# Expert jobs of 96 row slots, and four neighbouring rows of the experts' second matrix per partition

## The chip, the cores and the metric

The kernel runs on one core of a Trainium2 chip. The metric is the device time of one execution in microseconds; the median of several runs is compared. The core has a tensor engine (TensorE, "PE" in the profile, with its loads of stationary operands shown apart as "PEld"), a vector engine (VectorE, "DVE"), a scalar engine (ScalarE, "ACT"), GpSimd ("POOL") and SyncE ("SP"), which here only issues transfers. Sixteen DMA engines move data between HBM and the on-chip memory (SBUF, 128 partitions).

## The reference, cut to what matters

One step of a two-layer decoder on 256 prompt rows and 8 sample rows of width 1024, all in f32. Layer 0 is an HGRN2 recurrence followed by a dense SwiGLU with 3584 inner columns. Layer 1 is a short gated convolution followed by a SwiGLU of 8 experts, of which each row uses two:

```python
def moe_swiglu(x, router, w1, w3, w2):
    logits = (xt @ router).astype(F32)
    top_v, top_i = lax.top_k(logits, TOP_K)          # TOP_K = 2 of 8
    gates = jax.nn.softmax(top_v, axis=-1)
    combine = jnp.sum(jax.nn.one_hot(top_i, N_EXPERTS, dtype=F32) * gates[..., None], axis=1)
    for e in range(N_EXPERTS):
        out = out + combine[:, e:e + 1] * swiglu(xt, w1[e], w3[e], w2[e]).astype(F32)
```

`swiglu(x, w1, w3, w2)` is `(silu(x @ w1) * (x @ w3)) @ w2`, with `w1` and `w3` of 1024 x 3584 and `w2` of 3584 x 1024. A residual sum and a last RMSNorm follow.

## The kernel before

Every weight passes once from HBM through `raw` (three buffers of 128 x 4096 f32, each in two halves) and is split by ScalarE into a high part `whi` (line 887 in the expert stage) and by VectorE into a low part `wlo` (line 1020), both fp32r. A product then is three matmuls: high by high, high by low, low by high. A piece is half a buffer, 128 x 2048. SP issues the load of a half (line 332) as soon as the low part of that half's last content is made. The expert stage keeps six pieces split ahead; the semaphore `used` counts those that TensorE has done with.

The expert stage routes the 264 rows, gives each row a rank within each of its two experts, and scatters the normed rows into `xg_rows` in HBM (GpSimd, line 582), where each expert has `SLOTS = 3 * P` row slots: three jobs of up to 128 rows. `jobs` (line 290) runs the first job of each expert in order, eight in all; a second or third job is run only where `flag` says that an expert has more than 128 or 256 rows (lines 1609 to 1612). Both HBM buffers, `xg_rows` and `y_rows`, are filled with zeros beforehand, in twelve transfers issued by SP between the weight loads of the dense SwiGLU (`zero_rows`, line 403).

A job on TensorE: the rows of the job are loaded as `xg`, eight transposes (`turn_rows`, line 2130) put them into PSUM with the model columns on the partitions, ScalarE and VectorE copy them out as `xgh` and `xgl` (lines 926, 1576). For the first expert the rows come instead from matmuls with a selection matrix `pm` (line 2101). Then seven blocks of 512 inner columns follow. In each, `up_m` runs twice (banks 0 and 1, for `w1` and `w3`): 24 matmuls with `xgh` or `xgl` stationary and 512 columns of a weight piece moving (lines 2120 to 2122). ScalarE makes `hs = silu` (line 942), VectorE `hx = hs * bank 1` (line 1639), four transposes turn `hx` (`turn`, line 2151; `hx` stationary, the identity moving), ScalarE and VectorE copy the result out as `hth` and `htl` (lines 959, 1655), and `down_m` runs 24 matmuls with these stationary and 512 columns of the `w2` piece moving (line 2166), which add up in two banks over the whole job. TensorE's order is written out so that the transposes of a block stand between the two `up_m` of the next. At the end of a job ScalarE copies the sum into `ybuf` (line 987) and writes it to `y_rows`; after the last job GpSimd gathers each row's two results (line 590), and VectorE and ScalarE combine and norm them (lines 1688 to 1699).

Of the kernel before, what the change touches and what calls it, by code (L numbers as in the profile page):

```python
# [32 lines left out]
def build(nc, x_prompt, x_sample, state_hgrn, state_conv, norm_mix, norm_ffn, norm_final,  # L33
# [29 lines left out]
    SLOTS = 3 * P  # L63
# [8 lines left out]
    with ExitStack() as ctx:  # L72
# [78 lines left out]
        for g_ in range(2):  # L151
# [30 lines left out]
            R0, ("xs", [P, TT, D], F32), ("xgh", [P, DT, P], F32R), ("xgl", [P, DT, P], F32R),  # L182
            ("xg", [P, D], F32), ("hs", [P, FW], F32), ("hx", [P, FW], F32),
            ("hth", [P, 4, P], F32R), ("htl", [P, 4, P], F32R))
# [6 lines left out]
            ("cnt", [P, E], F32), ("flag", [P, NS + 8], I32), ("idx", [P, 2, TT], I32), ("pm", [P, TT, P], F32))  # L191
# [10 lines left out]
        assert FILL * (FB - 1) == E * SLOTS and FILL % (2 * P) == 0  # L202
# [87 lines left out]
        def jobs(eng, head, body):  # L290

            head(0, 0, 0)
            with eng.Fori(0, E - 1) as e:
                body(e, e, e * SLOTS, True)
            body(E - 1, E - 1, (E - 1) * SLOTS, False)  # L300
            more = eng.value_load(flag[0:1, NS:NS + 1], min_val=0, max_val=1)
            with eng.If(more > 0):
                count = eng.alloc_register("jobs_done")
                eng.reg_mov(count, E)
                with eng.Fori(1, 3) as c:
                    with eng.Fori(0, E) as e:
                        col = c * E + e
                        here = eng.value_load(flag[0:1, bass.ds(col, 1)], min_val=0, max_val=1)
                        with eng.If(here > 0):
                            k = eng.snap(count, min_val=E, max_val=3 * E)  # L310
                            head(k, e, e * SLOTS + c * P)
                            body(k, e, e * SLOTS + c * P, False)
                            eng.reg_add(count, count, 1)
                            eng.nop()
                        eng.end_ifs()
                        eng.nop()
            eng.end_ifs()
# [3 lines left out]
        def _(sp):  # L321
# [79 lines left out]
            def zero_rows(dst, i):  # L401

                sp.dma_start(dst[bass.ds(i * FILL, FILL), :].rearrange("(p r s) n -> p r (s n)", p=P, s=2),
                             zeros[:, :].unsqueeze(1).to_broadcast([P, FILL // P // 2, 2 * D])
                             ).then_inc(sem("zero_filled"), 16)
# [20 lines left out]

            def rows_in(k, row):
                sp.wait_ge(sem("dispatched"), 2 * TT * 16)
                sp.wait_ge(sem("xg_turned"), k)
                sp.dma_start(xg[:, :], xg_rows[bass.ds(row, P), :]).then_inc(sem("xg_loaded"), 16)  # L430
# [9 lines left out]
            def body(k, e, row, ahead):  # L440

                n = k * JOB + C_MOE
                with sp.Fori(0, FB - 1) as i:
                    m = n + i * 3 + 2
                    cols = bass.ds(i * FW + FW, FW)
                    chunk(m, expert(moe_w1, e, 0, DT)[:, :, cols], 2)
                    chunk(m + 1, expert(moe_w3, e, 0, DT)[:, :, cols], 0)
                    chunk(m + 2, expert(moe_w2, e, i * 4, 4), 1)
                if ahead:
# [3 lines left out]
                    chunk(n + (JOB + 1), expert(moe_w2, e, 4 * (FB - 1), 4), 1)  # L453
                else:
                    chunk(n + (JOB - 1), expert(moe_w2, e, 4 * (FB - 1), 4), 2)
# [141 lines left out]
        def _(act):  # L597
# [324 lines left out]
            def gathered(k):  # L922
# [3 lines left out]
                a.activation(xgh[:, :, :].rearrange("p (j d) s -> p j (d s)", j=2), Q[1][:, 2:4, :],  # L926
# [12 lines left out]
            def silu(nth, last):  # L939
                act.wait_ge(used, last)  # L940
                act.wait_ge(sem("hx_ready"), nth + 1)
                a.activation(hs[:, :], Q[0][:, 0, :], ACT.Silu).then_inc(sem("hs_ready"), 1)
# [9 lines left out]
            def body(k, e, row, ahead):  # L952
# [34 lines left out]
                a.activation(ybuf[:, :].rearrange("p (j n) -> p j n", j=2), Q[1][:, 0:2, :], ACT.Copy  # L987
                             ).then_inc(sem("y_copied"), 1)
                act.wait_ge(sem("y_copied"), k + 2)
                act.dma_start(y_rows[bass.ds(row, P), :], ybuf[:, :]).then_inc(sem("y_stored"), 16)  # L990
# [17 lines left out]
        def _(dve):  # L1008
# [564 lines left out]
            def gathered(k):  # L1573
# [3 lines left out]
                                Q[1][:, 2:4, :],  # L1577
# [7 lines left out]
            for t in range(TT):  # L1585
                v.tensor_scalar(pm[:, t, :], iota[:, :], 1.0, tk[:, 13, t:t + 1], ALU.add, ALU.is_equal
# [21 lines left out]
            for c in (1, 2):  # L1608
                then(v.tensor_scalar(flag[:, c * E:(c + 1) * E], cnt[:, :], float(P * c), None,
                                     ALU.is_gt))  # L1610
            then(v.tensor_reduce(tk[:, 2, 0:1], cnt[:, :], AX.X, ALU.max))
            then(v.tensor_scalar(flag[:, NS:NS + 1], tk[:, 2, 0:1], float(P), None, ALU.is_gt))
# [23 lines left out]
            def mul(nth, last):  # L1636
                dve.wait_ge(used, last)
                dve.wait_ge(sem("hs_ready"), nth + 1)
                v.tensor_tensor(hx[:, :], hs[:, :], Q[0][:, 1, :], ALU.mult
# [9 lines left out]
            def body(k, e, row, ahead):  # L1649
# [3 lines left out]
                def low(nth):  # L1653
                    dve.wait_ge(sem("hth_ready"), nth + 1)
                    v.tensor_tensor(htl[:, :, :].rearrange("p a s -> p (a s)"), Q[0][:, 2, :],  # L1655
# [49 lines left out]
        def _(pe):  # L1705
# [391 lines left out]
            for t in range(TT):  # L2097
                r = rows[t]
                pe.wait_ge(sem("xs_ready"), t + 1)
                for d in range(DT):  # L2100
                    mm = t_.matmul(Q[1][:, 2 + d // 4, P * (d % 4):P * (d % 4 + 1)],  # L2101
# [133 lines left out]
```

## Time and profile before

| | us |
|---|---|
| median of three runs | 1589.92 |
| lowest and highest | 1587.15, 1593.22 |
| the profiled execution | 1587.53 |
| its span, first to last instruction | 1585.8 |

| engine | busy in the span |
|---|---|
| TensorE matmul | 1499.7 us, 95% |
| TensorE loads | 1307.8 us, 82% |
| VectorE | 1239.5 us, 78% |
| ScalarE | 954.3 us, 60% |
| GpSimd | 66.5 us, 4% |
| DMA | 484.49 MB, mean 306 GB/s |

A row of the profile names the line, the engine, the operation, the tile written and those read, and their shapes. For a matmul the tiles read are the moving one first and the stationary one second; a load (`LDWEIGHTS`) names the same. The duration of one matmul (about 0.39 us) is longer than the distance to the next (0.23 us), since they are pipelined: the distance is what counts. The chain of waits goes back from the last instruction and gives each piece the time that it added to the end. Waits tell for whom an engine stood idle. Windows give busy time by stretch; "PEclk" is the granted share of TensorE's 2.4 GHz.

### The profile page before, as it was taken

Reading aid. Unit: us, or ns where it says so; the run is one execution under the profiler, and the core shown is the slowest. Engines: PE = TensorE matmul, PEld = TensorE weight load, DVE = VectorE, ACT = ScalarE, POOL = GpSimd, SP = SyncE. Lnnn points to the kernel's source line nnn. Section 1 sums busy time; section 2 is a strip of 40 time slices with the busy share of each in tenths; the row PEclk is TensorE's granted clock in tenths of the full one; section 3 lists DMA queues with packets and bytes.
Section 4 is the critical chain, followed back from the end, with each engine's and each line's share of the span. In section 5 each row is a group of like instructions: output and inputs, shape, how many; then the busy total and the mean of one; then the engine's idle time right before and its main releaser. Section 6 shows DMA issues by size and latency. Waiting matters only on the chain.

```text
span 1585.8 us, 23285 instructions
## 1 busy us (share of the span) xinstructions
PE 1499.7 (95%) x8758; PEld 1307.8 (82%) x8759; DVE 1239.5 (78%) x886; ACT 954.3 (60%) x671; POOL 66.5 (4%) x61
## 2 busy tenths in 40 slices
PE   6998699999989979999999999999999999999992
PEld 5987689999979978888888888888888888888881
DVE  5898665655657759888888888888888888888883
ACT  4644244334334347777777777777777777777761
POOL 1033400000000011000000000000000000000001
PEclk9999899999989989999999999999999999999997
DMA  7645377888726539999999999999999999999962
GB/s 269 194 154 163 124 280 268 297 312 312 248 102 200 167 99 400 395 393 374 377 380 370 377 379 370 377 384 360 389 375 362 383 382 357 385 381 362 380 240 96
DMA packets 212938, 484.49 MB, mean 306 GB/s; under 512 B 8810, under 2 KB 26314, under 8 KB 209820
## 3 DMA queue, kind: packets, MB, share of 16 engines
q1 hardware_dynamic: 209080, 473.67, 82.4%
q10 hardware_dynamic: 2532, 5.84, 1.0%
q0 software_dynamic: 1280, 4.33, 0.7%
q8 instruction: 33, 0.54, 0.1%
q14 instruction: 13, 0.11, 0.0%
HBM read 446.45 MB, written 37.40 MB: 305 GB/s over the span
## 4 chain that ended last, share of the span: by engine, by line
PE 82%; DVE 4%; issue 1%; ACT 1%; DMA 1%; POOL 0%; POOLq 0%; ACTq 0%; DVEq 0%
PE Q L2166 20%; PE Q L2122 13%; PE Q L2120 13%; PE Q L2121 13%; PE Q L1737 7%; PE Q L1738 7%; PE Q L1739 7%; PE Q L2151 2%; DVE wlo L1020 1%; DVE sr L1054 0%; PE Q L2101 0%; DMA back<-y_rows,idx 0%; PE Q L2130 0%; DVE xl L1046 0%; DVE xn L1041 0%
## 5 line engine op out<-in xcount | busy, mean ns | idle before, releaser
L1020 DVE TENSOR_TENSOR wlo<-raw,whi 128x2048 fp32r<-128x2048 f32 x414 | 940.3, 2289 | 207.0 <-ACT whi L887 121.1
L887 ACT ACTIVATE whi<-raw 128x2048 fp32r<-128x2048 f32 x336 | 643.1, 1921 | 185.0 <-PE Q L2122 85.4
L2120 PE MATMUL Q<-whi,xgh 128*128 128x512 f32 x896 | 357.5, 399 | 2.4 <-issue 2.4
L2122 PE MATMUL Q<-whi,xgl 128*128 128x512 f32 x896 | 353.8, 395 | 0.0
L2121 PE MATMUL Q<-wlo,xgh 128*128 128x512 f32 x896 | 352.8, 394 | 0.0
L1737 PE MATMUL Q<-xh,whi 128*128 128x264 f32 x1024 | 298.3, 291 | 14.7 <-DVE xl L1046 6.3
L1738 PE MATMUL Q<-xl,whi 128*128 128x264 f32 x1024 | 295.5, 289 | 0.0
L1739 PE MATMUL Q<-xh,wlo 128*128 128x264 f32 x1024 | 294.1, 287 | 0.0
L1737 PEld LDWEIGHTS Q<-xh,whi 128*128 128x128 f32 x1024 | 197.4, 193 | 17.4 <-issue 15.6
L2120 PEld LDWEIGHTS Q<-whi,xgh 128*128 128x128 f32 x896 | 169.3, 189 | 38.1 <-issue 2.6
L2122 PEld LDWEIGHTS Q<-whi,xgl 128*128 128x128 f32 x896 | 169.2, 189 | 37.6
L2121 PEld LDWEIGHTS Q<-wlo,xgh 128*128 128x128 f32 x896 | 169.3, 189 | 36.6
L1738 PEld LDWEIGHTS Q<-xl,whi 128*128 128x128 f32 x1024 | 197.4, 193 | 0.4
L1739 PEld LDWEIGHTS Q<-xh,wlo 128*128 128x128 f32 x1024 | 196.8, 192 | 0.0
L2166 PE MATMUL Q<-whi,hth 128*128 128x512 f32 x448 | 176.3, 393 | 1.4 <-DVE htl L1655 1.4
L2166 PE MATMUL Q<-whi,htl 128*128 128x512 f32 x448 | 177.0, 395 | 0.0
L2166 PE MATMUL Q<-wlo,hth 128*128 128x512 f32 x448 | 176.0, 393 | 0.0
L608 ACT ACTIVATE whi<-raw 128x2048 fp32r<-128x2048 f32 x42 | 80.0, 1912 | 86.0 <-PE Q L1739 83.7
L823 ACT ACTIVATE whi<-raw 128x2048 fp32r<-128x2048 f32 x36 | 68.8, 1911 | 90.2 <-PE Q L1739 90.2
L2166 PEld LDWEIGHTS Q<-whi,hth 128*128 128x128 f32 x448 | 84.5, 189 | 20.0 <-DVE htl L1655 1.6
L2166 PEld LDWEIGHTS Q<-wlo,hth 128*128 128x128 f32 x448 | 84.2, 188 | 19.3
L2166 PEld LDWEIGHTS Q<-whi,htl 128*128 128x128 f32 x448 | 84.4, 188 | 18.4
(231 smaller groups left out, 1099.1 us busy)
## 6 DMA issues: line engine op xcount, KB each, us to landing
raw<-in_moe_w SPq DMA_DIRECT2D x336, 1024.0 KB, 7.6
raw<-in_ffn_w SPq DMA_DIRECT2D x42, 1024.0 KB, 6.9
raw<-in_hgrn_w_in SPq DMA_DIRECT2D x16, 1024.0 KB, 6.4
xg_rows<-zeros SPq DMA_DIRECT2D x6, 2048.0 KB, 10.8
y_rows<-zeros SPq DMA_DIRECT2D x6, 2048.0 KB, 10.8
raw<-in_conv_w_in SPq DMA_DIRECT2D x12, 1024.0 KB, 6.0
st<-in_state_hgrn SPq DMA_DIRECT2D x8, 512.0 KB, 4.4
raw<-in_hgrn_w_out SPq DMA_DIRECT2D x4, 1024.0 KB, 5.1
```

Of the source, the lines that this page charges most:

```text
L608: a.activation(whi[:, buf, :], raw[:, slot, PW * half:PW * (half + 1)], ACT.Copy).then_inc(hi_done, 1)
L823: a.activation(whi[:, base % SPLIT, :], raw[:, n % RAW, PW * (base % 2):PW * (base % 2 + 1)], ACT.Copy).then_inc(hi_done, 1)
L887: a.activation(bufs(q)[0], raw[:, n % RAW, PW * (q % 2):PW * (q % 2 + 1)], ACT.Copy).then_inc(hi_done, 1)
L1020: v.tensor_tensor(low, raw[:, slot, PW * half:PW * (half + 1)], high.bitcast(F32), ALU.subtract).then_inc(lo_done, 1)
L1737: t_.matmul(out, w[wslice], xhi, start=start, stop=False, **kw)
L1738: t_.matmul(out, w[wslice], xlo, start=False, stop=False, **kw)
L1739: return t_.matmul(out, lo[wslice], xhi, start=False, stop=stop, **kw)
L2120: t_.matmul(out, xgh[:, kt, :], high[:, w], start=(kt == 0), stop=False)
L2121: t_.matmul(out, xgh[:, kt, :], low[:, w], start=False, stop=False)
L2122: mm = t_.matmul(out, xgl[:, kt, :], high[:, w], start=False, stop=(kt == DT - 1))
L2151: mm = t_.transpose(Q[0][:, 2, P * c:P * (c + 1)], hx[:, P * c:P * (c + 1)], ident[:, :])
L2166: mm = t_.matmul(out, lhs[:, f, :], rhs[:, w], start=(begin and f == 0 and lhs is hth and rhs is high), stop=(last and f == 3 and lhs is h ...
```

## The change

A job has 96 row slots in place of 128 (`CAP`). `SLOTS` becomes 288, a job's rows lie `c * CAP` behind the expert's first, and the flags compare with 96 and 192. `xgh`, `xgl`, `hth`, `htl` and `pm` are 96 wide, the outputs of the matmuls and the copies of `hs`, `hx`, `ybuf` and `xg` use 96 partitions, and the transposes use a 96 x 96 identity. The zero fill has 384 rows a transfer, each row written on its own. A partition of a `w2` chunk gets the four rows 4p to 4p + 3 of the block's 512 in place of rows p, 128 + p, 256 + p and 384 + p, so that a half chunk has 8 KB of adjacent memory per partition; `turn` takes every fourth column of `hx` to match.

```diff
     JOB = 3 * FB
-    SLOTS = 3 * P
+    CAP = 96
+    SLOTS = 3 * CAP
...
-            R0, ("xs", [P, TT, D], F32), ("xgh", [P, DT, P], F32R), ("xgl", [P, DT, P], F32R),
+            R0, ("xs", [P, TT, D], F32), ("xgh", [P, DT, CAP], F32R), ("xgl", [P, DT, CAP], F32R),
             ("xg", [P, D], F32), ("hs", [P, FW], F32), ("hx", [P, FW], F32),
-            ("hth", [P, 4, P], F32R), ("htl", [P, 4, P], F32R))
+            ("hth", [P, 4, CAP], F32R), ("htl", [P, 4, CAP], F32R))
...
-                            head(k, e, e * SLOTS + c * P)
-                            body(k, e, e * SLOTS + c * P, False)
+                            head(k, e, e * SLOTS + c * CAP)
+                            body(k, e, e * SLOTS + c * CAP, False)
...
-                sp.dma_start(dst[bass.ds(i * FILL, FILL), :].rearrange("(p r s) n -> p r (s n)", p=P, s=2),
-                             zeros[:, :].unsqueeze(1).to_broadcast([P, FILL // P // 2, 2 * D])
+                sp.dma_start(dst[bass.ds(i * FILL, FILL), :].rearrange("(p r) n -> p r n", p=P),
+                             zeros[:, 0:D].unsqueeze(1).to_broadcast([P, FILL // P, D])
                              ).then_inc(sem("zero_filled"), 16)
...
+            def expert_w2(e, i):
+
+                return moe_w2[0].rearrange("e (i p k) n -> p (e i) k n", p=P, k=4)[:, bass.ds(e * FB + i, 1), :, :
+                                           ].rearrange("p i k n -> p (i k) n")
+
             def rows_in(k, row):
                 sp.wait_ge(sem("dispatched"), 2 * TT * 16)
                 sp.wait_ge(sem("xg_turned"), k)
-                sp.dma_start(xg[:, :], xg_rows[bass.ds(row, P), :]).then_inc(sem("xg_loaded"), 16)
+                sp.dma_start(xg[0:CAP, :], xg_rows[bass.ds(row, CAP), :]).then_inc(sem("xg_loaded"), 16)
...
-                    chunk(m + 2, expert(moe_w2, e, i * 4, 4), 1)
+                    chunk(m + 2, expert_w2(e, i), 1)
...
-                a.activation(hs[:, :], Q[0][:, 0, :], ACT.Silu).then_inc(sem("hs_ready"), 1)
+                a.activation(hs[0:CAP, :], Q[0][0:CAP, 0, :], ACT.Silu).then_inc(sem("hs_ready"), 1)
...
-                    a.activation(hth[:, :, :].rearrange("p a s -> p (a s)"), Q[0][:, 2, :], ACT.Copy
+                    a.activation(hth[:, :, :].rearrange("p a s -> p (a s)"), Q[0][:, 2, 0:4 * CAP], ACT.Copy
...
-            then(v.tensor_scalar(flag[:, NS:NS + 1], tk[:, 2, 0:1], float(P), None, ALU.is_gt))
+            then(v.tensor_scalar(flag[:, NS:NS + 1], tk[:, 2, 0:1], float(CAP), None, ALU.is_gt))
...
-                        out = Q[0][:, bank, :]
+                        out = Q[0][0:CAP, bank, :]
...
-                    mm = t_.transpose(Q[1][:, 2 + d // 4, P * (d % 4):P * (d % 4 + 1)],
-                                      xg[:, P * d:P * (d + 1)], ident[:, :])
+                    mm = t_.transpose(Q[1][:, 2 + d // 4, CAP * (d % 4):CAP * (d % 4 + 1)],
+                                      xg[0:CAP, P * d:P * (d + 1)], ident[0:CAP, 0:CAP])
...
-                        mm = t_.transpose(Q[0][:, 2, P * c:P * (c + 1)], hx[:, P * c:P * (c + 1)],
-                                          ident[:, :])
+                        mm = t_.transpose(Q[0][:, 2, CAP * c:CAP * (c + 1)],
+                                          hx[0:CAP, :].rearrange("p (m k) -> p k m", k=4)[:, c, :],
+                                          ident[0:CAP, 0:CAP])
...
-                                out = Q[1][:, j, :]
+                                out = Q[1][0:CAP, j, :]
```

The other copies out of PSUM (`xgh`, `xgl`, `htl`, `ybuf`), the product `hx` and the write of `y_rows` change in the same way.

## Rows read from the trace of the kernel before

**Rows 1.** Windows: stretch, its length, busy of each engine (instructions), clock, DMA.
```profile
250.00:300.00 50.00, 50.00 (x413) 50.00 (x413) 30.15 (x17) 19.89 (x12) 0.00 (x0) 1.00 0.81 283
1200.00:1300.00 100.00, 100.00 (x448) 81.83 (x447) 87.00 (x48) 73.64 (x49) 0.00 (x0) 1.00 1.02 376
```
**Rows 2.** Waits of TensorE, 600 to 1549 us: total, times, longest.
```profile
PE Q L2151 <- DVE hx L1639: 0.2, 1, 0.2
```
**Rows 3.** The chain, 640 to 1500 us: start, us, what.
```profile
995.54 5.53 PE Q L2166 x24
1012.59 5.53 PE Q L2166 x24
...
1183.94 0.87 PE Q L2130 x8
```
**Rows 4.** The chain around one block's four transposes of hx.
```profile
1504.32 0.23 PE Q L2122
1504.55 0.44 PE Q L2151 x4
1504.99 0.23 PE Q L2120
```
**Rows 5.** Timeline: start, us, instruction; other transposes, and two early matmuls.
```profile
77.79 0.60 PE L1797 MATMUL Q<-ident,vpad 128*96 128x128 f32 x4
...
544.20 1.03 PE L2049 MATMUL Q<-ident,cg 128*10 128x128 f32 x8 [1.55 <-DVEq L1506]
...
13.51 1.03 PE L1722 MATMUL Q<-ident,brows 16*128 16x16 f32 x8
...
21.24 0.42 PE L1738 MATMUL Q<-xl,whi 128*128 128x264 f32 x1
...
21.46 0.42 PE L1739 MATMUL Q<-xh,wlo 128*128 128x264 f32 x1
```
**Rows 6.** Groups by line: loads of hx, cg; and of the router (min/median/max ns).
```profile
L2151 PEld LDWEIGHTS Q<-ident,hx 128*128 128x128 f32 x200 | 25.0, 140 | 6.6
...
L2049 PEld LDWEIGHTS Q<-ident,cg 128*10 128x10 f32 x8 | 0.6, 86 | 1.9 <-issue 1.7
...
L2062 PEld LDWEIGHTS Q<-router,xT x48: 85/192/193, 562.4 to 575.6; 128*128 128x128 f32 x32, 128*8 128x8 f32 x16
```
**Rows 7.** The chain at the router's first half.
```profile
562.69 1.97 PE Q L2062 x24
```
**Rows 8.** Before the first expert: one us of L2101, the chain's end, the first matmul.
```profile
587.00:588.00 1.00, 1.00 (x12) 1.00 (x11) 1.00 0.00 0
...
591.77 1.23 DVE xgl L1576
...
593.10 0.58 PE L2120 MATMUL Q<-whi,xgh 128*128 128x512 f32 x1 [2.42 <-issue]
```
**Rows 9.** Groups by line and form, ACT and DVE: busy us, mean ns, idle before.
```profile
L959 ACT ACTIVATE hth<-Q 128x512 fp32r<-128x512 f32 x56 | 33.2, 594 | 9.0 <-PE Q L2151 9.0
...
L926 ACT ACTIVATE xgh<-Q 128x1024 fp32r<-128x1024 f32 x8 | 8.2, 1026 | 18.2 <-PE Q L2130 12.6 <-PE Q L2101 5.6
...
L1655 DVE TENSOR_TENSOR htl<-Q,hth 128x512 fp32r<-128x512 f32 x56 | 38.3, 683 | 5.9 <-ACT hth L959 5.9
...
L1576 DVE TENSOR_TENSOR xgl<-Q,xgh 128x1024 fp32r<-128x1024 f32 x8 | 9.7, 1217 | 2.4 <-ACT xgh L926 2.4
```
**Rows 10.** The chain at the end: the last write of y_rows.
```profile
1558.91 3.05 DMA y_rows<-ybuf
```
**Rows 11.** Timeline of SP in the dense stage: two zero fills of y_rows.
```profile
259.12 0.57 SPq L403 DMA_DIRECT2D y_rows<-zeros  x1
...
294.17 0.57 SPq L403 DMA_DIRECT2D y_rows<-zeros  x1
```
**Rows 12.** Transfers into raw: time to land, SP's waits (640 to 1500), a window.
```profile
DMA to landing us min/median/max: 5.1/7.2/8.3
...
SPq L332 <- DVE wlo L1020: 649.3, 301, 4.6
...
600.00:606.00 6.00, 6.00 (x27) 4.90 (x26) 5.90 (x6) 5.51 (x5) 0.15 (x1) 1.00 1.03 416
```
**Rows 13.** The last blocks, transfers ended: a window, and the chain's last full group.
```profile
1540.00:1550.00 10.00, 10.00 (x45) 8.12 (x45) 3.78 (x4) 1.57 (x1) 0.00 (x0) 1.00 0.01 2
...
1544.58 5.53 PE Q L2166 x24
```

More of the change, by code:

```diff
@@ L190, in build @@
             ("iote", [P, E], F32), ("base", [P, E], F32),
-            ("cnt", [P, E], F32), ("flag", [P, NS + 8], I32), ("idx", [P, 2, TT], I32), ("pm", [P, TT, P], F32))
+            ("cnt", [P, E], F32), ("flag", [P, NS + 8], I32), ("idx", [P, 2, TT], I32), ("pm", [P, TT, CAP], F32))
         W2_AT = max(o, conv_end)
@@ L201, in build @@
         FILL = E * SLOTS // (FB - 1)
-        assert FILL * (FB - 1) == E * SLOTS and FILL % (2 * P) == 0
+        assert FILL * (FB - 1) == E * SLOTS and FILL % P == 0
         def bufs(q):
@@ L452, in body @@
                     chunk(n + JOB, expert(moe_w3, e + 1, 0, DT)[:, :, 0:FW], 0)
-                    chunk(n + (JOB + 1), expert(moe_w2, e, 4 * (FB - 1), 4), 1)
+                    chunk(n + (JOB + 1), expert_w2(e, FB - 1), 1)
                 else:
-                    chunk(n + (JOB - 1), expert(moe_w2, e, 4 * (FB - 1), 4), 2)
+                    chunk(n + (JOB - 1), expert_w2(e, FB - 1), 2)
                 if not isinstance(k, int):
@@ L925, in gathered @@
                 act.wait_ge(used, k * (2 * JOB) + (M0 - 4))
-                a.activation(xgh[:, :, :].rearrange("p (j d) s -> p j (d s)", j=2), Q[1][:, 2:4, :],
+                a.activation(xgh[:, :, :].rearrange("p (j d) s -> p j (d s)", j=2), Q[1][:, 2:4, 0:4 * CAP],
                              ACT.Copy).then_inc(sem("xgh_ready"), 1)
@@ L986, in body @@
                 act.wait_ge(sem("y_stored"), k * 16 + 16)
-                a.activation(ybuf[:, :].rearrange("p (j n) -> p j n", j=2), Q[1][:, 0:2, :], ACT.Copy
+                a.activation(ybuf[0:CAP, :].rearrange("p (j n) -> p j n", j=2), Q[1][0:CAP, 0:2, :], ACT.Copy
                              ).then_inc(sem("y_copied"), 1)
                 act.wait_ge(sem("y_copied"), k + 2)
-                act.dma_start(y_rows[bass.ds(row, P), :], ybuf[:, :]).then_inc(sem("y_stored"), 16)
+                act.dma_start(y_rows[bass.ds(row, CAP), :], ybuf[0:CAP, :]).then_inc(sem("y_stored"), 16)
                 if not ahead:
@@ L1576, in gathered @@
                 v.tensor_tensor(xgl[:, :, :].rearrange("p (j d) s -> p j (d s)", j=2),
-                                Q[1][:, 2:4, :],
+                                Q[1][:, 2:4, 0:4 * CAP],
                                 xgh[:, :, :].rearrange("p (j d) s -> p j (d s)", j=2).bitcast(F32),
@@ L1585, in _ @@
             for t in range(TT):
-                v.tensor_scalar(pm[:, t, :], iota[:, :], 1.0, tk[:, 13, t:t + 1], ALU.add, ALU.is_equal
+                v.tensor_scalar(pm[:, t, :], iota[:, 0:CAP], 1.0, tk[:, 13, t:t + 1], ALU.add, ALU.is_equal
                                 ).then_inc(sem("pm_ready"), 1)
@@ L1608, in _ @@
             for c in (1, 2):
-                then(v.tensor_scalar(flag[:, c * E:(c + 1) * E], cnt[:, :], float(P * c), None,
+                then(v.tensor_scalar(flag[:, c * E:(c + 1) * E], cnt[:, :], float(CAP * c), None,
                                      ALU.is_gt))
             then(v.tensor_reduce(tk[:, 2, 0:1], cnt[:, :], AX.X, ALU.max))
-            then(v.tensor_scalar(flag[:, NS:NS + 1], tk[:, 2, 0:1], float(P), None, ALU.is_gt))
+            then(v.tensor_scalar(flag[:, NS:NS + 1], tk[:, 2, 0:1], float(CAP), None, ALU.is_gt))
             dve.sem_inc(sem("hx_ready"), 1)
@@ L1638, in mul @@
                 dve.wait_ge(sem("hs_ready"), nth + 1)
-                v.tensor_tensor(hx[:, :], hs[:, :], Q[0][:, 1, :], ALU.mult
+                v.tensor_tensor(hx[0:CAP, :], hs[0:CAP, :], Q[0][0:CAP, 1, :], ALU.mult
                                 ).then_inc(sem("hx_ready"), 1)
@@ L1654, in low @@
                     dve.wait_ge(sem("hth_ready"), nth + 1)
-                    v.tensor_tensor(htl[:, :, :].rearrange("p a s -> p (a s)"), Q[0][:, 2, :],
+                    v.tensor_tensor(htl[:, :, :].rearrange("p a s -> p (a s)"), Q[0][:, 2, 0:4 * CAP],
                                     hth[:, :, :].rearrange("p a s -> p (a s)").bitcast(F32),
@@ L2100, in _ @@
                 for d in range(DT):
-                    mm = t_.matmul(Q[1][:, 2 + d // 4, P * (d % 4):P * (d % 4 + 1)],
+                    mm = t_.matmul(Q[1][:, 2 + d // 4, CAP * (d % 4):CAP * (d % 4 + 1)],
                                    xs[0:r, t, P * d:P * (d + 1)], pm[0:r, t, :],
```

## The prediction

> **What bounds the kernel now.** I read the stages first. In the expert stage, from 600 us to the end of the last job, TensorE is busy without a gap at the full granted clock while VectorE stands at 87% and ScalarE at 74%; in the dense feed-forward stage TensorE is at 100% too [rows 1]. Then the waits: over 949 us of expert work TensorE waited 0.2 us in all [rows 2]. So the expert stage, 60% of the span, is a plain sum of TensorE instructions, and no saving on another engine counts there unless it shortens that sum.
>
> The chain of work gives the prices. The 24 matmuls of the second matrix take 5.53 us, 0.2304 us each, and one such group follows the last after 17.05 us (995.54, 1012.59). A block is 72 matmuls and four transposes of `hx`: 72 x 0.2304 = 16.59, which leaves 0.46 for the four. A job adds eight transposes of gathered rows, 0.87 us, 0.109 each [rows 3]. The chain has the four `hx` transposes at 0.44, 0.11 each [rows 4]. Check: 56 blocks x 17.05 + 7 x 0.87 = 961 us, the length of the stage.
>
> What sets each? A matmul has a load of its stationary operand and a stream of its moving one. For matmuls the stream is the 512 columns of an expert matrix, which the change leaves alone. For transposes, `hx` or `xg` is stationary (128 columns) and the identity moves (128 columns, 96 after). Transposes with 96 and with 10 stationary columns and 128 moving ones took 0.60 us for four (three steps and a last one of 0.273: 0.109 a step) and 1.03 for eight (0.108): the width of the stationary operand doesn't show. With 16 moving columns, at 13.5 us, eight took 1.03: also 0.109, but at half pace (matmuls of 264 columns come 0.22 us apart at 21 us and 0.121 later, though the clock column has 1.00 there), where 128 moving columns would take twice 0.109 [rows 5]. So the step follows the moving columns.
>
> **The change part by part.** The sum is made against the profiled execution: 1587.53 us, of which the span is 1585.8. The median of the three runs, 1589.92, is 2.4 above it.
>
> Jobs. Each expert must still need one job. The reference's routing over its inputs gives the experts 61, 72, 67, 80, 67, 63, 66 and 52 rows; the largest, 80, is under 96. No second jobs arise, and the flag test against 96 stays false.
>
> Matmuls, 56 x 72 = 4032. Stationary `xgh`, `xgl`, `hth`, `htl` get 96 columns; the moving 512 and the count stay. Price: nothing, from the transposes above, where 96 and 128 stationary columns cost the same. Bounds: the dense stage has 413 matmuls of 264 columns in 50 us, 0.121 each [rows 1]; with 0.2304 at 512 that is 0.44 ns a column and 5 ns besides. If the 5 ns went with the stationary width, a quarter of it x 4032 = -5 us. If all above 512 columns at 2.4 GHz (213.3 ns) did, -17 us. Above: nothing in the rows makes a narrower load dearer, +0.
>
> Gather transposes, 7 x 8 = 56: 96 moving columns in place of 128, 0.109 x 96/128 = 0.082, so -27 ns each: -1.5 us (bound 0).
>
> `hx` transposes, 56 x 4 = 224. The moving side falls to 0.082 as well, but the stationary side now reads every fourth element of `hx`, 16 bytes apart, which no row shows for TensorE. The load of 128 contiguous columns has 140 ns, that of 10 columns 86: 54 ns for 118 columns, about 58 for 128, hidden behind the stream. The router's f32 loads of the same 128 columns have 192 ns [rows 6], and 24 router matmuls, 16 of them with 128 stationary columns and all with only 8 moving ones, took 1.97 us: 0.082 each, or 0.123 if the eight narrow ones were free [rows 7]. So a load about twice as long sets a step of 0.08 to 0.12 by itself. Bounds: 0.082 if the strided load stays hidden (224 x -27 ns = -6.0 us); 4 x 58 = 232 ns if a load takes four times as long (224 x 0.123 = +27.5). I take today's 0.109, in the middle of the 0.082 to 0.123 which the twice longer load gives: a contiguous stream already arrives at 0.44 ns a column where 2.4 GHz would allow 0.417, so a read that steps over three of four elements is likelier slower than not. Term: 0.
>
> A page speaks to this: the Trainium skill (SBUF — State Buffer, the note on cachelines) says that SBUF is read in 16-byte lines, and that at least two accesses must fall on one line for full bandwidth. `hx` at a step of four f32 has one access a line. It gives no size of the penalty. By that rule the -6.0 is lost; if it did not hold, it is gained. No row of this case shows it.
>
> The first dispatch, 48 matmuls at L2101, also gets 96 moving columns, but it is plain f32 with 128 stationary columns: at the full clock about 11 pairs pass in a us [rows 8], near the router's pace, set by the load. Term 0. Behind it stand one ACT copy and one DVE subtraction over 1024 columns which become 768. From 0.594 and 1.026 us for 512 and 1024 columns ACT pays 0.84 ns a column, from 0.683 and 1.217 DVE 1.04 [rows 9]: -0.22 and -0.27. They end at 593.00, the first expert matmul starts at 593.10, so both count. At the very end `hth` and `htl` of the last block go from 512 to 384 columns with TensorE waiting: -0.11 and -0.13. In all 55 other blocks the two lie beside matmuls: nothing, and if TensorE ever waited for them they are shorter, not longer. `ybuf`, `hs` and `hx` keep their columns and lose partitions only: nothing. The last write of `y_rows` moves 96 rows: 3.05 us [rows 10], taken as unchanged (bound -0.5). Together -0.7.
>
> Zero fill: 12 transfers on SP's queue shrink from 2 MB to 1.5, with runs of 4 KB. They stand between weight loads of the dense stage, which issue 35 us apart per block [rows 11] while TensorE is at 100% [rows 1]: nothing. SP issues as many instructions as before.
>
> Second matrix in runs of 8 KB: the same bytes, 16 KB of adjacent memory per partition in two halves; every user (`hi`, `lo`, matmul) keeps its shape, and the transposes' new step matches rows to it. The transfers land in 7.2 us (5.1 to 8.3), and SP waited for DVE to free a buffer 301 times, 649 us in all [rows 12], never TensorE for a transfer. A block needs 6.29 MB in 17.05 us, 369 GB/s; at 600 to 606 us the engines moved 416. The slack covers it: 0. Cover gone, it costs what a block's transfers exceed 17.05 us.
>
> Sum: 0 - 1.5 + 0 - 0.7 = -2.2 us: 1585.3 by the profiled execution (1587.7 by the median). I give 1585.
>
> **The rivals.** *Strided loads cost nothing* (0.28): -6.0 more, 1579. For it: the load's 58 ns leaves room under 82. Against it: the spacing of the reads above.
>
> *Strided loads four times as long* (0.12), the one on the slow side: L2151, four loads a block, on TensorE's own sum; 1585.3 + 27.5 = 1613. It decides from where the load's part passes 0.109, about twice the present 58 ns; three times is 0.174, +15 us.
>
> *Matmuls follow the stationary width too* (0.12): -5 to -17 on the sum, 1568 to 1580, about 1574. For it: the pace of 0.2304 doesn't come from the transfers, since it is the same from 1540 us on, when they have ended [rows 13], and the load is the part left. Against it: the transposes with 10 stationary columns.
>
> *The second matrix's transfers become the bound* (0.04): its third of a block would have to fall under 320 GB/s (2.1 MB in the 6.5 us that 4.2 MB at 400 leave); at 300, +25 us.
>
> *The edit doesn't do what it says* (0.06): transposes keep their step with 96 moving columns, or the 8 KB runs are cut up as before. Only -0.7 is left, 1587.
>
> **How the numbers follow.** Forecast 0.36, which with a remainder of 0.02 makes 1. The range takes in the forecast, the free load, the edit without effect and most of the faster matmuls, and a part of the slow loads: 1571 to 1598. This kernel's measurement tells about 0.5%, 8 us, from no change. Faster by more: most of the matmul case and, as -8.2 lies on the line, half of the free loads: 0.25. Slower: loads or transfers, 0.16. Within: 0.59.
>
> **What would show it.** In the trace after: a block's period (17.05 if `hx` transposes keep their price, 16.95 if free, 17.5 if fourfold), `L2151 x4` in the chain, its load's mean against 140 ns, eight gather transposes at 0.66, the 24 matmuls at 5.53, the first expert matmul 0.5 us sooner after L2101, packets fewer by 256 a block. The prediction falls if matmuls with 96 stationary columns are not at 0.2304, or if TensorE waits for transfers.

## The result: 0.2% slower

| | before | after |
|---|---|---|
| median, us (20 executions each, taken in turn) | 1589.58 | 1592.72 |
| lowest and highest | 1587.03, 1593.22 | 1587.52, 1595.63 |
| span of the profiled execution | 1585.8 | 1589.4 |

The ratio is 1.002, with a 95% interval of 1.0012 to 1.0028: +3.1 us. That is inside the range (1571 to 1598) and inside 0.5%, where most of the chance lay, but the forecast point said -2.2 us and the interval excludes a gain. The range held because it is wide; the direction was wrong, and something of 5 to 6 us was mis-sized.

### The profile page after: what moved, and what is told of

The parts are those of the page before. It is cut to its first block, busy times and chain, and to the rows that moved or that the text cites. A ratio compares the mean times of both kernels' runs of the same rounds, so it can differ in the third digit from the quotient of the medians.

```text
span 1589.4 us, 23285 instructions
## 1 busy us (share of the span) xinstructions
PE 1503.9 (95%) x8758; PEld 1204.8 (76%) x8759; DVE 1233.0 (78%) x886; ACT 947.7 (60%) x671; POOL 64.6 (4%) x61
## 2 busy tenths in 40 slices
DMA packets 199658, 476.23 MB, mean 300 GB/s; under 512 B 8810, under 2 KB 26314, under 8 KB 185276
## 4 chain that ended last, share of the span: by engine, by line
PE 83%; DVE 3%; issue 1%; ACT 1%; DMA 1%; POOL 0%; POOLq 0%; ACTq 0%; DVEq 0%
PE Q L2173 20%; PE Q L2126 13%; PE Q L2127 13%; PE Q L2128 13%; PE Q L1743 7%; PE Q L1744 7%; PE Q L1745 7%; PE Q L2157 2%; DVE wlo L1026 1%; PE Q L2107 1%; DVE sr L1060 0%; DMA back<-y_rows,idx 0%; DVE xl L1052 0%; DVE xn L1047 0%; PE Q L2136 0%
## 5 line engine op out<-in xcount | busy, mean ns | idle before, releaser
L2126 PE MATMUL Q<-whi,xgh 128*96 128x512 f32 x896 | 356.9, 398 | 1.9 <-issue 1.9
L2127 PE MATMUL Q<-wlo,xgh 128*96 128x512 f32 x896 | 353.8, 395 | 0.0
L2128 PE MATMUL Q<-whi,xgl 128*96 128x512 f32 x896 | 353.5, 395 | 0.0
L2126 PEld LDWEIGHTS Q<-whi,xgh 128*96 128x96 f32 x896 | 147.3, 164 | 61.6 <-issue 2.1
L2128 PEld LDWEIGHTS Q<-whi,xgl 128*96 128x96 f32 x896 | 145.2, 162 | 63.3
L2127 PEld LDWEIGHTS Q<-wlo,xgh 128*96 128x96 f32 x896 | 145.4, 162 | 59.5
L2173 PE MATMUL Q<-whi,hth 128*96 128x512 f32 x448 | 176.4, 394 | 1.2 <-DVE htl L1661 1.2
L2173 PE MATMUL Q<-wlo,hth 128*96 128x512 f32 x448 | 176.4, 394 | 0.0
L2173 PE MATMUL Q<-whi,htl 128*96 128x512 f32 x448 | 175.9, 393 | 0.0
L2173 PEld LDWEIGHTS Q<-whi,hth 128*96 128x96 f32 x448 | 72.3, 161 | 32.3 <-DVE htl L1661 1.3
```

The costliest lines, as they stand in the source:

```text
L2126: t_.matmul(out, xgh[:, kt, :], high[:, w], start=(kt == 0), stop=False)
L2127: t_.matmul(out, xgh[:, kt, :], low[:, w], start=False, stop=False)
L2128: mm = t_.matmul(out, xgl[:, kt, :], high[:, w], start=False, stop=(kt == DT - 1))
L2173: mm = t_.matmul(out, lhs[:, f, :], rhs[:, w], start=(begin and f == 0 and lhs is hth and rhs is high), stop=(last and f == 3 and lhs is h ...
```

## The profile after

The page of the kernel after, its parts on engines and on packets:

```profile
PE 1503.9 (95%) x8758; PEld 1204.8 (76%) x8759; DVE 1233.0 (78%) x886; ACT 947.7 (60%) x671; POOL 64.6 (4%) x61
DMA packets 199658, 476.23 MB, mean 300 GB/s; under 512 B 8810, under 2 KB 26314, under 8 KB 185276
```

TensorE's loads shrank by 103 us (1307.8 before), VectorE's and ScalarE's busy time by 6.5 each, the packets by 13,280 (212,938 before). None of that is the bound; the matmuls' busy time went up, 1499.7 to 1503.9.

The chain of the kernel after (start us, its share us, what), in the order in which it runs:

```profile
583.65 8.78 PE Q L2107 x48
592.43 1.94 issue
594.37 0.71 PE Q L2126
...
705.53 0.66 PE Q L2136 x8
...
998.41 5.55 PE Q L2173 x24
...
1015.53 5.55 PE Q L2173 x24
...
1032.64 5.55 PE Q L2173 x24
...
1508.44 0.44 PE Q L2157 x4
...
1562.69 3.01 DMA y_rows<-ybuf
```

Against [rows 3, 4]: eight gather transposes 0.66 in place of 0.87, as forecast; four `hx` transposes 0.44, also as forecast; but the 24 matmuls of `down_m` take 5.55 in place of 5.53, and the groups follow at 17.12 and 17.11 in place of 17.05. The place of the loss can be read by comparing starts at the same piece: the first dispatch begins 0.21 us later than before, the transposes at 1508.44 stand 3.89 later than those at 1504.55, and the last write begins 3.78 later than the one at 1558.91 [rows 10]. So all is lost between 584 and 1508 us, while the gather transposes give back 1.5 there. The waits of TensorE from 600 to 1549 us have no row in the kernel after: nothing new is waited for.

The groups of instructions from 640 to 1500 us of the kernel after (busy us, mean ns, idle before):

```profile
L2157 PEld LDWEIGHTS Q<-ident,hx 96*128 96x128 f32 x200 | 31.8, 209 | 5.1
L2157 PE MATMUL Q<-ident,hx 96*128 96x96 f32 x200 | 30.3, 274 | 0.0
L2136 PEld LDWEIGHTS Q<-ident,xg 96*128 96x128 f32 x56 | 5.4, 141 | 1.1
L2136 PE MATMUL Q<-ident,xg 96*128 96x96 f32 x56 | 5.8, 245 | 0.0
L2126 PEld LDWEIGHTS Q<-whi,xgh 128*96 128x96 f32 x800 | 131.1, 164 | 52.9
L1661 DVE TENSOR_TENSOR htl<-Q,hth 128x384 fp32r<-128x384 f32 x50 | 27.5, 551 | 0.0
L965 ACT ACTIVATE hth<-Q 128x384 fp32r<-128x384 f32 x50 | 23.9, 479 | 0.0
```

The rows of L2157 and L2136 are a control pair: both transposes have 96 partitions, 128 stationary and 96 moving columns. Only the step between the stationary elements differs. The contiguous load takes 141 ns, the one that reads every fourth f32 takes 209 (140 before, [rows 6]).

**A finer ruler.** The trace gives durations to 0.01 us; what is wanted here is some 0.02 us a block. So I took the starts of all matmuls in the trace and averaged, over some 50 blocks, the time from the start of one part to the start of the one behind it: the first `up_m` (24 matmuls), the four `hx` transposes ("turn"), the first matmul of the second `up_m` ("next"), its other 23, and `down_m` (24). In ns:

| kernel | first `up_m` | turn | next | other 23 | `down_m` | block |
|---|---|---|---|---|---|---|
| before | 5580 | 355.5 | 314 | 5267 | 5530 | 17046 |
| before again (e11) | 5579 | 356.1 | 312 | 5267 | 5532 | 17046 |
| after | 5571 | 390.0 | 284 | 5317 | 5551 | 17113 |
| e1, e9: 96 slots only | 5568 | 276.5, 277.8 | 285 | 5321 | 5544 | 16995 |
| e2: layout only | 5573 | 389.6 | 316 | 5274 | 5541 | 17094 |
| e3: after, tiles 128 wide | 5577 | 389.2 | 319 | 5271 | 5541 | 17097 |
| e5: e1 with tiles and dispatch 128 wide | 5577 | 276.5 | 317 | 5274 | 5535 | 16979 |
| e6, e10: as e5, tiles 96 wide | 5569 | 276.2, 277.1 | 285 | 5322 | 5543 | 16995 |
| e7: 8 KB runs, contiguous `hx` | 5578 | 354.7 | 315 | 5266 | 5532 | 17046 |

Two traces of one kernel differ by under 1 ns in a block (before and e11, e1 and e9, e6 and e10), so steps of 10 ns are safe. Over 56 blocks the 67 ns that the kernel after takes longer make +3.8 us.

Inside the turn the trace shows where the time goes (means of 42 or 43 blocks, in ns). The three steps from transpose to transpose are 109, 108 and 109 before, 85, 118 and 120 after, and 86, 82 and 82 in e1, where 96 columns are read contiguously; from the start of the last transpose to the start of the next matmul it is 28, 66 and 28. So with the stride the second and third steps take 118 to 120 ns, and the three together are 4 ns shorter than before; what makes the turn longer is the last gap, +38.

## Experiments

My first theory after the result: the strided load costs the transposes what their 96 moving columns give, and there is a second loss in the matmuls with 96 stationary columns. Its rivals: the 8 KB runs disturb the reads of TensorE, or the loss lies in the dispatch.

**One half alone.** e1 keeps 96 slots and takes the old layout:

```diff
-                    chunk(m + 2, expert_w2(e, i), 1)
+                    chunk(m + 2, expert(moe_w2, e, i * 4, 4), 1)
...
-                                          hx[0:CAP, :].rearrange("p (m k) -> p k m", k=4)[:, c, :],
+                                          hx[0:CAP, P * c:P * (c + 1)],
```

> Jobs of 96 slots, second matrix laid out as before, hx turned from adjacent columns. Theory W (a stationary operand of 96 columns makes every matmul 0.8 ns slower, 0.2312 in place of 0.2304 us): a group of 24 stays at 5.55 us, the four hx transposes fall from 0.44 to 0.33, a block takes 17.00 us. Theory L (the second matrix in 8 KB runs slows the matmuls): a group of 24 back to 5.53, a block 16.94. Both: load of hx back from 209 to about 141 ns. Against the kernel before: W -2.4 (blocks) -1.5 -0.7 and, if the first dispatch stays longer at the lower clock, +2.5: about -2 us; L about -8, or -5 with the clock.

Measured: 1586.79 against 1588.05 of before, 0.9993 [0.9982, 1.0005]; block 16,995 ns. e2 keeps the new layout and goes back to 128 slots:

```diff
-    CAP = 96
-    SLOTS = 3 * CAP
+    CAP = 128
+    SLOTS = 3 * P
```

> Jobs of 128 slots, second matrix in 8 KB runs, hx read at a step of four. Theory W: a group of 24 at 5.53, four hx transposes at 0.44, a block 17.05 us, the time that of the kernel before within 1 us. Theory L: a group of 24 at 5.55, a block 17.11, +3.7 us. Both: the mean load of hx about 209 ns in place of 140.

Measured: 1591.42, 1.0025 [1.0016, 1.0034]; block 17,094 ns. Groups of L2157 in e1 and then in e2, from 640 to 1500 us, and their chains:

```profile
L2157 PEld LDWEIGHTS Q<-ident,hx 96*128 96x128 f32 x200 | 22.3, 140 | 8.0
1006.49 0.33 PE Q L2157 x4
1012.38 5.54 PE Q L2173 x24
```

```profile
L2157 PEld LDWEIGHTS Q<-ident,hx 128*128 128x128 f32 x200 | 32.0, 205 | 3.9
1008.60 0.47 PE Q L2157 x4
1014.58 5.54 PE Q L2173 x24
```

The slots give (0.33 for four transposes), the layout takes (0.47). Neither theory holds alone: e1 came out as W had it (16,995 for 17.00), e2 nearer to L (17,094 for 17.11), because the stride costs time between the first transpose and the next matmul, which neither theory counted. With the stride, 96 moving columns save nothing in the turn (390.0 in the kernel after, 389.6 in e2). Since "layout" is two edits, e7 has the 8 KB runs with contiguous loads (this kernel pairs the rows of the second matrix with the wrong columns of `hx`; work and sizes are those of before):

```diff
-    CAP = 96
-    SLOTS = 3 * CAP
+    CAP = 128
+    SLOTS = 3 * P
...
-                                          hx[0:CAP, :].rearrange("p (m k) -> p k m", k=4)[:, c, :],
+                                          hx[0:CAP, P * c:P * (c + 1)],
```

> The kernel before with the second matrix in 8 KB runs, but hx turned from adjacent columns, so that rows and columns of the second product no longer match and the result is another; the work is the same. It prices the layout without the strided loads: transposes' stretch 0.356 and load 140 ns as before. If the 8 KB runs themselves slow the matmuls, the down group is 5.541 in place of 5.530 and a block about 17.06; if the strided loads do it, a block is 17.05.

Measured: 1586.08 in one execution, block 17,046 ns, every part of it within 3 ns of before. The 8 KB runs cost nothing and give nothing; e7 to e2 is the stride alone, +47 ns a block or +2.6 us.

**How far must a load step to be slow?** e8 is the kernel after with a step of two f32, 8 bytes, in each half of `hx` (again with columns that don't match their rows):

```diff
-                                          hx[0:CAP, :].rearrange("p (m k) -> p k m", k=4)[:, c, :],
+                                          hx[0:CAP, 2 * P * (c // 2):2 * P * (c // 2 + 1)].rearrange("p (m k) -> p k m", k=2)[:, c % 2, :],
```

> The changed kernel with hx read at a step of two f32 (8 bytes) in place of four; rows and columns of the second product don't match, the result is another. Theory S (a read is slower only where no two elements lie in the same 16 bytes): load 141 ns, stretch of the four transposes 0.276 as with adjacent columns, a block 17.00. Rival (the load slows with any step): load between 141 and 209, stretch up to 0.39.

```profile
L2157 PEld LDWEIGHTS Q<-ident,hx 96*128 96x128 f32 x200 | 31.6, 208 | 5.2
```

208 ns at a step of two, 209 at four, 140 at one; turn 384 ns, block 17,101, 1590.51 us in one execution. The step of two costs nearly all that the step of four does, against Theory S. The Trainium skill (SBUF — State Buffer, the note on cachelines) asks for at least two accesses on each 16-byte line for full bandwidth, which a step of two f32 has, and names four f32 as how far one can stride for free. The trace disagrees with both for these loads (208 and 209 ns against 140), and the measurement decides.

**Width of the stationary operand.** e3 is the kernel after with `xgh`, `xgl`, `hth`, `htl` 128 wide (columns 96 to 127 zero) and outputs of 128 partitions:

```diff
+    W = 128
...
-            R0, ("xs", [P, TT, D], F32), ("xgh", [P, DT, CAP], F32R), ("xgl", [P, DT, CAP], F32R),
+            R0, ("xs", [P, TT, D], F32), ("xgh", [P, DT, W], F32R), ("xgl", [P, DT, W], F32R),
...
-                        out = Q[0][0:CAP, bank, :]
+                        out = Q[0][0:W, bank, :]
```

> The changed kernel, but the four stationary tiles are 128 columns wide (columns 96 to 127 are zeros) and the matmuls write 128 partitions; everything else as changed. Theory W: a group of 24 back to 5.53, a block 17.05, 3.7 us faster than the changed kernel. Theory L: 5.55 and 17.11 stay, no gain.

Measured: 1591.78, 1.0018 [1.0006, 1.003]; block 17,097 against 17,113 of after. That is far from the 17.05 of Theory W. Narrow operands make the block 16 ns longer, not shorter: the first matmul behind the transposes gains 35, the 23 others lose 46, `down_m` loses 10 and the first `up_m` gains 6. e5 and e6 repeat the pair where nothing is strided. e6 is e1 with the dispatch of before (below), e5 is e6 with tiles 128 wide, by the edit of e3.

> Jobs of 96 slots; second matrix as before; hx turned from adjacent columns by transposes of 96 moving columns; stationary tiles and matmul outputs 128 wide (upper 32 columns zero); first dispatch with 128 moving columns. By the sum of the terms measured so far: the stretch of the transposes falls from 0.356 to 0.276 us a block, first and later matmuls as before, a block 16.97 in place of 17.05: -4.4 us, gather transposes -1.5, the copies around -0.7: -6.6 us against the kernel before, ratio 0.996, clock at 1.00 about 3 us after the dispatch begins. If the slowdown of the matmuls comes from the 96-slot form itself and not from the stationary width, the second up group stays at 5.32 after its first matmul and the gain is about 4 us.

> As the run before, but the stationary tiles 96 columns wide: contiguous hx, old layout of the second matrix, dispatch with 128 moving columns. Theory W: per block first matmul after the transposes 0.285 in place of 0.314, the other 23 of that group 5.32 in place of 5.27, the down group 5.54 in place of 5.53: 16.99 us a block, about 1.5 us slower than the run before. Theory C: compared with the same kernel with 96 moving columns in the dispatch, the 48 dispatch matmuls fall from 8.9 to 7.2 us.

Measured: e5 1582.82, 0.996 [0.9946, 0.9974]; e6 1583.61, 0.9963 [0.995, 0.9976]. Blocks 16,979 and 16,995: +16 again. In time the two can't be told apart, only in the distances (their expectations, 16.97 and 16.99, both came). Three more widths followed. e12 is the kernel after with `W = 64` (only 64 rows of a job are computed), e14 is e5 with `W = 112`, and e15 is e5, tiles still 128 wide, with only 96 of their columns used:

```diff
-                        t_.matmul(out, xgh[:, kt, :], high[:, w], start=(kt == 0), stop=False)
+                        t_.matmul(out, xgh[:, kt, 0:CAP], high[:, w], start=(kt == 0), stop=False)
```

> The changed kernel with the stationary tiles 64 columns wide, so that only 64 rows of each job enter the matmuls and the result is another; transposes, copies and loads of weights as changed. If the pace of the matmuls follows the width of the stationary tile, the first matmul after the transposes falls by another 0.03 us from 0.284 and the other 23 of that group rise from 5.32 by the same 0.05 again; if 96 is a single odd case, they stay within 5.27 to 5.32.

> As the narrow combined kernel, but stationary tiles and outputs 112 wide (columns 96 to 111 zero). If the pace follows the width smoothly: the 23 matmuls after the first at 5.30, between 5.27 of 128 and 5.32 of 96, a block about 16.985. If the pace depends on the load length beating with something else, any value from 5.25 to 5.35, with another pattern within the group.

> As the combined kernel with tiles 128 wide at the same addresses, but the matmuls load only their first 96 columns and write 96 partitions. Theory W (the width of the load sets the pace): 5.32 for the 23 matmuls and a block of 16.995 us, as in the narrow combined kernel. Rival (the addresses of the tiles set it): 5.27 and 16.98, as in the combined kernel.

One execution each: 1581.95, 1587.79 and 1590.39 us. Their blocks are 16,935 (e12, with strided transposes), 17,042 and 17,081 ns. The block less its turn, divided by 72, is the mean distance of a matmul: 229.8 ns at 64 columns, 230.9 at 80 (e17, below), 232.0 at 128 (e5), 232.2 at 96 (e6), 232.9 at 112, and 233.4 for 96 columns out of tiles 128 wide. None of the three met its expectation: in e12 the first matmul behind the transposes took 291 ns, not less than 284, and the other 23 fell to 5252; in e14 the 23 took 5329, not 5300; in e15 they took 5372, outside both theories. e15 differs from e6 only in where the tiles and their columns lie in memory: loads of the same 96 columns, 162 ns in both, and 86 ns a block between them. It differs from e5, with the same tiles, in the width of the loads: 102 ns a block. So both the place and the width move the distance, it doesn't follow the width in a line, and what sets it is open.

**The first dispatch.** e4 is the kernel after with the 48 matmuls at L2107 back at 128 moving columns:

```diff
-... ("pm", [P, TT, CAP], F32))
+... ("pm", [P, TT, P], F32))
...
-                    mm = t_.matmul(Q[1][:, 2 + d // 4, CAP * (d % 4):CAP * (d % 4 + 1)],
+                    mm = t_.matmul(Q[1][:, 2 + d // 4, P * (d % 4):P * (d % 4 + 1)],
```

> The changed kernel, but the first dispatch (48 matmuls at L2107) moves 128 columns as before. Theory C (96 moving columns keep TensorE less active, so its clock rises later): the clock is at 1.00 again from about 587 us and the 48 take about 7.3 us, about 2.5 us faster than the changed kernel. Theory C' (where the clock rises is chance from run to run): the same spread of switch times as the changed kernel, no difference in the median.

Measured: 1591.0, 1.0015 [1.0005, 1.0025]; by the ratios 0.8 us under the kernel after, where Theory C asked for 2.5 and the two intervals overlap almost wholly; the block is the same, 17,113. The 48 matmuls in the chain, and windows of TensorE, in the kernel before and then in the kernel after (stretch, length, busy with matmuls, granted clock, DMA share, GB/s); the dispatch of the latter starts at 583.65:

```profile
583.44 7.26 PE Q L2101 x48
...
586.00:588.00 2.00, 2.00 (x18) 0.88 0.00 0
588.00:590.00 2.00, 2.00 (x19) 1.00 0.00 0
...
594.00:596.00 2.00, 2.00 (x6) 0.50 0.94 357
596.00:598.00 2.00, 2.00 (x9) 0.82 1.03 420
```

```profile
586.00:588.00 2.00, 2.00 (x12) 0.50 0.00 0
588.00:590.00 2.00, 2.00 (x11) 0.50 0.00 0
590.00:592.00 2.00, 2.00 (x18) 0.99 0.70 53
...
596.00:598.00 2.00, 2.00 (x6) 0.50 1.02 418
598.00:600.00 2.00, 2.00 (x6) 0.50 1.03 424
600.00:602.00 2.00, 2.00 (x10) 0.93 1.05 424
```

TensorE comes to the dispatch at 1.2 GHz. With 128 moving columns it is back at 2.4 GHz 3.1 us after the start and the 48 matmuls take 7.26 us; with 96 it is back after 6.4, and they take 8.78. After the pause behind them the clock is at 1.2 GHz again, for the first expert matmuls: up to 13.3 us after the start in the one kernel, 16.6 in the other. Is that the width, or chance? e9 and e10 repeat e1 and e6, which differ only in the dispatch.

> The kernel of the first experiment once more (96 slots, contiguous hx, 96 moving columns in the first dispatch). Theory C: the 48 dispatch matmuls take 8.7 to 8.9 us again, the clock is back at 1.00 only some 6 us after they begin, and the time is 2 to 5 us above that of its twin below with 128 moving columns. Theory C' (chance): the two twins take the same time within 1 us, and either may show the short or the long rise.

> The twin: the same kernel with 128 moving columns in the first dispatch, for the second time. Theory C: the 48 take 7.2 us, clock at 1.00 about 3 us after they begin, 2 to 5 us faster than the twin above. Theory C': no difference. A third outcome of 128 columns with the long rise, as in the layout run, is possible in either.

> The kernel before, profiled again. Theory C: 48 dispatch matmuls in about 7.3 us, clock back after about 3 us; a block 17.05 us to within 0.005. Theory C': anything between 7.2 and 8.9.

e9 1584.41, 0.9974 [0.9962, 0.9986]; e10 1584.15, 0.9966 [0.9956, 0.9976]; e11 1588.71 in one execution. In the six traces with 96 moving columns the clock rose 6.1 to 6.7 us after the start and the 48 matmuls took 8.6 to 8.9 us; in ten of twelve with 128 it rose after 2.8 to 3.1 and they took 7.1 to 7.3. The other two (e7, e14) took 8.6 and 8.7 with a rise at 6.0, so the width shifts the odds and doesn't decide. The Trainium skill (TensorE: Matmul & The Clock Gate, on the warmup) says that the number of matmuls before the rise varies between runs of one kernel. These two agree in so far as the same 48 matmuls had both rises in different kernels; of the kernels traced twice none showed both.

The traces give the price. From the start of the first of the 48 to the start of the first `hx` transpose TensorE took 30.18 us in the kernel after and 27.75 in e4, 29.92 in e9 and 27.72 in e10, 30.31 in e1 and 27.66 in e6: 2.2 to 2.7 us for the narrow dispatch. The two wide ones with the late rise took 30.15 (e7) and 29.91 (e14), so it is the late rise that costs, at either width. One narrow trace, e12, took only 28.69: there the clock was back for the expert matmuls after 13.1 us, not 16.6. In the device time the gain is not clear of noise: e9 and e10 differ by 0.3 us in the medians (1.3 by the ratios), where Theory C asked for 2 to 5; after and e4 by 0.8 and e1 and e6 by 4.8, both by the ratios, since the two of each pair were not taken in turn with each other.

**Fewer slots still.** The fullest expert of this input has 80 rows. e13 and e17 are one kernel: e6 with `CAP = 80` and `SLOTS = 3 * P`. e16 is the same with 80 moving columns in the dispatch.

> Jobs of 80 slots (the fullest expert has 80 rows, so each still needs one job): transposes with 80 moving columns, stationary tiles of 80 columns, hx from adjacent columns, second matrix as before, first dispatch with 128 moving columns. If 96 is an odd case and narrower tiles are faster, as 64 was: a block about 16.83 us or less, some 12 us faster than the kernel before. If the pace stays that of 96: transposes' stretch 0.276 - 4 x 0.013 = 0.22, a block 16.94, gather 0.55 for eight, 8 to 9 us faster. If transposes with 80 columns are bound by their loads (58 ns, under 68): no change to this.

> The kernel of 80 slots with 80 moving columns in the first dispatch. Theory C: the 48 dispatch matmuls take 8.6 to 8.9 us or more, clock back at 1.00 after 6 us or later, and the time is 2 to 5 us above the twin below. Theory C' (chance): the same time within 1 us.

> The kernel of 80 slots with 128 moving columns in the first dispatch, once more: ratio to the kernel before 0.992 again. Theory C: 48 dispatch matmuls in 7.2 us; theory C': no faster than the twin above.

Measured: e13 1575.51, 0.9917 [0.9902, 0.9932]; e17 1574.23, 0.9912 [0.9898, 0.9925]; e16 1578.06, 0.9925 [0.9911, 0.9938]. The chain of e17, and its windows at the dispatch; then those windows of e16, whose dispatch starts at 586.57:

```profile
584.47 7.18 PE Q L2110 x48
...
1001.67 0.28 PE Q L2160 x4
1007.48 5.52 PE Q L2176 x24
1018.53 0.28 PE Q L2160 x4
1024.34 5.52 PE Q L2176 x24
```

```profile
588.00:590.00 2.00, 2.00 (x18) 1.00 0.00 0
```

```profile
586.57 10.71 PE Q L2107 x48
588.00:590.00 2.00, 2.00 (x11) 0.50 0.00 0
590.00:592.00 2.00, 2.00 (x12) 0.50 0.00 0
592.00:594.00 2.00, 2.00 (x10) 0.50 0.21 24
594.00:596.00 2.00, 2.00 (x11) 0.50 0.87 224
```

Four transposes take 0.28 and a group follows the last after 16.86; the block, by the same averages, is 16,859 ns in all three, 188 under before: x 56 = 10.5 us, near the first of e13's two expectations (16.83): at 80 columns the matmuls are faster too. The gather transposes (0.55 for eight in place of 0.87, seven times) bring 2.2 more; that is 12.7 of the 13 to 14 us. With 80 moving columns the 48 matmuls of the dispatch never left 1.2 GHz in e16, 10.71 us against 7.18, which goes further than Theory C, and from the start of the dispatch to the first `hx` transpose it is 31.02 us against 27.46. The medians are 3.8 us apart, though the intervals of the two ratios overlap. The version with 128 moving columns beats the kernel before by 0.8 to 0.9% and, by the ratios, the kernel after by 1.0 to 1.1%; but it has no row to spare: an input that sends 81 rows to one expert runs a second job of seven blocks, some 118 us by the block of 16.86 (an estimate; no run had such an input).

## Why the prediction went wrong

Right, each by its own row:
- No second job; no wait of TensorE for a transfer, with 256 packets fewer a block (e1 to after, 213,994 to 199,658, is 56 x 256) and transfers that land as before (7.4 us in the median, 7.5 before).
- The stage is the sum of TensorE's distances, and a loss appears there one for one.
- Gather transposes 0.66, -1.5 us. Copies: `xgh` 813 ns, `xgl` 948, `hth` 479, `htl` 551, within 0.02 us of the working. Zero fill and 8 KB runs: 0.
- The strided load has 209 ns in place of 140, within the twice longer load that the working took, and neither *free* (16.95) nor *fourfold* (17.5) came.

Wrong are three terms of the sum that were put at 0: the first dispatch, +2.4 us, the `hx` transposes, +1.9, and the matmuls, +1.8. These are the steps that failed. No one of them turns the forecast's -2.2 into a clear loss; any two do.
- **First dispatch, term 0 (+2.4, the largest).** The rate at the full clock was judged rightly, but the term was read from a stretch at 2.4 GHz [rows 8], and the 48 matmuls begin at 1.2. From their start to the start of the first `hx` transpose it took 28.25 us before and 30.18 after, +1.9. e4, with the same shorter copies and the wide dispatch, took 27.75, so the copies gave their -0.5 and the late rise of the clock cost +2.4 (2.2 to 2.7 in the other pairs). The first expert matmul, forecast 0.5 us sooner, started 1.1 later from the start of the dispatch (9.66 to 10.72); in e4 it was 0.5 sooner (9.16).
- **`hx` transposes, term 0 (+1.9).** From the first of them to the next matmul it is 390.0 ns in place of 355.5, +34.5 x 56 = +1.9 us. The value of 0.109 a step was nearly right for the three steps between transposes, in part by luck: one of 85 and two of 118 to 120 average 108. The chain's 0.44, which the working used, hides the rest: it shows the four transposes, not the 38 ns more until the next matmul starts. The bound for a free load was wrong too: it counted four steps at -27 ns, -6.0 us, but there are three, and the 96 columns alone give 276.5 in place of 355.5 (e5), 79 ns a block or -4.4 us. Against that the stride costs 113 ns a block in jobs of 96 slots, 6.4 us; the working put it at 6.0, from the router's f32 loads (192 ns, near the 209).
- **Matmuls, term 0, "nothing in the rows makes a narrower load dearer, +0" (+1.8).** The 72 matmuls of a block take 33 ns more: 16 by the narrow tiles (e3 to after, and e5 to e6), 6 in `down_m` with the strided transposes (e5 to e3), and 11 between before and e5, whose 72 matmuls have the same shapes in both (not explained). 33 x 56 = +1.8 us. The upper bound had no reason but the lack of a row: the transposes with 10 stationary columns showed that width doesn't shorten a step of 0.109, and I read this as "width doesn't matter" for another kind of matmul. The rival *matmuls follow the stationary width too* fell at 96 columns by the same rows: it wanted 1.25 to 4 ns off each matmul, and they are 0.2 slower than 128 (e6, e5). At 80 and 64 columns 1.1 and 2.2 ns do come off.

The sum anew, from the starts in the traces of before and after: the dispatch begins 0.2 us later; from there to the first `hx` transpose +1.9 (2.4 - 0.5); from the first to the last `hx` transpose +2.0, where 1.9 + 1.8 - 1.5 by the terms would be +2.2; and from there to the end -0.5, of which -0.2 is the forecast for `hth` and `htl` and another -0.2 a last gather from `y_rows` that took 6.25 us in place of 6.42. Together +3.6, as the span grew. The forecast's terms that held (-2.2) are in it; the three zeros that weren't are +6.1, and -0.3 was in no term.

What stays open: why the distance of two matmuls of 512 columns moves between 229.8 and 233.4 ns with the width and place of the stationary operand, and in no steady order, and why the clock rises later with the narrow dispatch, and late in two of twelve traces with the wide one. That the rise costs is shown, and where the stride costs; why a distance of 0.23 us follows where the columns lie is not.

## What to carry to other kernels

Shrinking the moving side of a transpose from 128 to 96 columns paid here only where the stationary side was read contiguously (79 ns a block against none): don't buy a strided load with a merging of DMA runs that are hidden anyway. Price a group of instructions up to the start of the one behind it. A term set to zero needs a bound on both sides, above all where it is multiplied by 4032. Where an engine starts a stretch at its low clock, fewer columns there can cost more than they save: look at the granted clock on both sides of the edit.

## What the hardware showed that was not expected

- The load of 128 f32 columns for these transposes takes 140 ns contiguous and 205 to 209 at a step of two or of four elements; a step of two (208) is hardly cheaper than four (209). The steps between such transposes are 82 ns in the one case and up to 120 in the other (the kernel after).
- Matmuls with 512 moving columns differ by 1.2 ns in their distance by where their 96 stationary columns lie (232.2 packed, 233.4 in tiles 128 wide), and 112 columns are slower than 128 (232.9 against 232.0).
- With 128, 96 and 80 moving columns in the same 48 f32 matmuls TensorE was back at 2.4 GHz after about 3 us (ten of twelve traces), after 6.1 to 6.7 (six of six), and not before they ended (one trace).
